# A two-layer decoder trunk on one core: output turns of the delta rule a step later, squares kept at norm boundaries, weight splits elsewhere

## What is computed

```python
def rms_norm(x, w):
    return x * lax.rsqrt(jnp.mean(x * x, axis=-1, keepdims=True) + NORM_EPS) * w

for layer in range(2):
    h = h + 0.5 * rms_norm(swiglu(rms_norm(h, nw[0]), gate0, up0, down0), nw[1])
    hn = rms_norm(h, nw[2])
    mix = even_mixer(hn, ...) if layer == 0 else odd_mixer(hn, ...)   # both end in "@ w_out"
    h = h + rms_norm(mix, nw[3])
    h = h + 0.5 * rms_norm(swiglu(rms_norm(h, nw[4]), gate1, up1, down1), nw[5])
return h[:, 16:]

# a part of even_mixer: the gated delta rule, four heads of 128, over a scan of chunks
def step(s, xs):
    attn_n, u_n, w_n, qd_n, kd_n, gl_n = xs
    v_new = u_n - w_n @ s
    o = qd_n @ s + attn_n @ v_new
    s = s * gl_n[..., None, None] + kd_n.T @ v_new
    return s, o                       # later: rms_norm(o, norm_w) * silu(z)
```

## Time and profile before

| | |
|---|---|
| median of 3 runs | 2191.31 us (2188.11 to 2193.72) |
| profiled execution, its own time | 2191.5 us |
| its span, first to last instruction | 2189.7 us |
| PE busy | 2145.0 us (98%), 16006 matmuls |
| DVE busy | 1010.7 us (46%) |
| ACT busy | 763.9 us (35%) |
| POOL busy | 100.1 us (5%) |
| mean granted clock of PE | 0.992 |

### The profile page before, as it was taken

The page is one execution under the profiler, slowest core; times in us unless marked ns, Lnnn a source line. Parts: engine busy times, 40 slices in busy tenths (PEclk is TensorE's granted clock), DMA queues, the critical chain, the costliest instruction groups (busy, mean ns, idle before and its releaser), DMA issues.

```text
span 2189.7 us, 38299 instructions
## 1 busy us (share of the span) xinstructions
PE 2145.0 (98%) x16006; PEld 2026.2 (93%) x16006; DVE 1010.7 (46%) x1390; ACT 763.9 (35%) x1259; POOL 100.1 (5%) x97
## 2 busy tenths in 40 slices
PE   8999999999999999999999999999999999999998
PEld 7999999998998999999999999999998788888887
DVE  6444422667485464444236444412663346444423
ACT  5222222346435542223234222322453454222322
POOL 0000000100050200000000000000000020000000
PEclk9999999999999999999999999999999999999999
DMA  4333333321110223334313332431322122333232
GB/s 128 95 90 94 98 107 85 77 74 49 49 30 1 76 79 88 94 89 119 93 56 87 88 94 87 118 93 51 94 78 59 40 70 85 95 96 96 96 106 77
DMA packets 328974, 179.69 MB, mean 82 GB/s; under 512 B 15849, under 2 KB 323344, under 8 KB 328878
## 3 DMA queue, kind: packets, MB, share of 16 engines
q1 hardware_dynamic: 327520, 175.30, 27.4%
q0 software_dynamic: 1024, 2.86, 0.5%
q10 hardware_dynamic: 334, 0.14, 0.0%
HBM read 176.16 MB, written 2.12 MB: 81 GB/s over the span
## 4 chain that ended last, share of the span: by engine, by line
PE 93%; DVE 4%; ACT 1%; issue 1%; DMA 0%; DVEq 0%; SPq 0%; ACTq 0%
PE psum L608 69%; PE psum L620 10%; PE psum L808 6%; DVE w_hl L523 1%; PE psum L2390 1%; PE psum L1858 1%; PE psum L2929 1%; PE psum L1870 0%; DMA stage<-ffn_w_gate 0%; PE psum L2945 0%; PE psum L2940 0%; DVE rinv L1374 0%; PE psum L674 0%; PE psum L698 0%; PE psum L2449 0%
## 5 line engine op out<-in xcount | busy, mean ns | idle before, releaser
L608 PE MATMUL psum<-x_hl,w_hl 128*128 128x264 f32 (+1 forms) x9120 | 1243.5, 298 | 7.2 <-DVE w_hl L523 6.0
L608 PEld LDWEIGHTS psum<-x_hl,w_hl 128*128 128x128 f32 x9120 | 1184.6, 189 | 59.1 <-issue 7.9
L523 DVE TENSOR_TENSOR w_hl<-stage,w_hl 128x1024 fp32r<-128x1024 f32 (+1 forms) x310 | 398.5, 1285 | 346.6 <-ACT w_hl L516 346.6
L516 ACT ACTIVATE w_hl<-stage 128x1024 fp32r<-128x1024 f32 (+1 forms) x310 | 339.5, 1096 | 217.4 <-PE psum L608 95.7
L608 PE MATMUL psum<-acts,w_hl 128*128 128x264 f32 x2376 | 288.9, 284 | 0.0
L608 PEld LDWEIGHTS psum<-acts,w_hl 128*128 128x128 f32 x2376 | 288.6, 188 | 0.0
L1416 DVE TENSOR_TENSOR t_both<-psum,rinv 128x528 f32<-128x528 f32 (+1 forms) x88 | 61.9, 703 | 304.4 <-PE psum L608 304.4
L1228 ACT ACTIVATE acts<-t_both 128x528 f32 (+3 forms) x88 | 56.7, 644 | 401.2 <-DVE t_both L1419 401.2
L620 PE MATMUL psum<-x_hl,w_hl 128*128 128x264 f32 (+1 forms) x1344 | 173.8, 289 | 6.9 <-DVE w_hl L523 4.6
L620 PEld LDWEIGHTS psum<-x_hl,w_hl 128*128 128x128 f32 x1344 | 168.0, 191 | 9.8 <-DVE w_hl L523 5.0
L1410 DVE TENSOR_TENSOR t_both<-psum,rinv 128x528 f32<-128x528 f32 (+1 forms) x88 | 61.9, 703 | 181.3 <-PE psum L608 181.1
(11 more groups left out here) (347 smaller groups left out, 1294.7 us busy)
## 6 DMA issues: line engine op xcount, KB each, us to landing
stage<-ffn_w_gate SPq DMA_DIRECT2D x88, 512.0 KB, 3.7
stage<-ffn_w_up SPq DMA_DIRECT2D x88, 512.0 KB, 3.7
stage<-ffn_w_down SPq DMA_DIRECT2D x48, 704.0 KB, 4.6
stage<-odd_w_in SPq DMA_DIRECT2D x24, 512.0 KB, 3.7
stage<-ffn_w_down SPq DMA_DIRECT2D x22, 512.0 KB, 3.4
stage<-even_w_in SPq DMA_DIRECT2D x18, 512.0 KB, 3.7
stage<-even_w_out SPq DMA_DIRECT2D x8, 512.0 KB, 3.5
stage<-odd_w_out SPq DMA_DIRECT2D x8, 512.0 KB, 3.5
```

Of the source, the lines that this page charges most:

```text
L516: act.activation(weights(core.w_hl[:, slot.ring, 0, :], *kind), weights(core.stage[:, slot.stage, :], *kind), ACT.Copy).then_inc(core.w_hi, 1)
L523: dve.tensor_tensor(weights(core.w_hl[:, slot.ring, 1, :], *kind), weights(core.stage[:, slot.stage, :], *kind), weights(core.w_hl[:, slot ...
L608: op = pe.matmul(out, lhs, moving[:, moved, kt, t0:t0 + n], start=first and part + moved == 0, stop=last and part == 1)
```

## The change

Four things, in the functions that the diff names.

1. At every boundary, `pre_sum` of part 1 is made after channel tile 6 of slots 0 to 2 (`PRE_SUM_KT`), before the last 9 matmuls of that loop, not after them.
2. At the two boundaries after "out": PE takes channel tiles 0 to 3 of slot 0, then 0 to 3 of slot 1, then 4 and 5 of each, then 6 and 7 (`first_order`); it waits for slot 1's weights only when it comes to slot 1; part 1's sums stand after unit 14 and its spread after unit 20; `pre_sum` of part 0 comes after slot 2. The squares of pairs 1 to 3 go into `in_squares`, where each keeps its place, and DVE adds all three after the last remainders. The third weight split of part 0 comes after pair 3; the fourth stands before the wait for part 1's spread.
3. Delta rule: the output turn of chunk c-1 stands after the inner product of chunk c on PE; ACT copies the new values before it scales the output of chunk c-1; DVE gates chunk c-2 where it gated c-1, and before the state's additions; the remainders of the attention's output are all made after the loop.
4. The decay of the last chunk's queries moves from `chunk_gates` to just before the last 128-token chunk's first inverse, and the weight split at item 4 moves to item 10.

```diff
 SUMS_UNIT, SPREAD_UNIT = 4, 9
+FIRST_UNITS = {"down": (4, 9), "out": (14, 20)}
+PRE_SUM_KT = 6
+
+def first_order(kind):
+    groups = [[0, 1, 2, 3], [4, 5], [6, 7]] if kind == "out" else [[kt] for kt in range(DT)]
+    return [(u, kt) for group in groups for u in range(2) for kt in group]
...
+def pair_squares(core, phase, pair):
+    return core.in_squares[:, 2 * pair:2 * pair + 2, :] if phase.kind == "out" else core.t_both
...
-    pe.wait_ge(k.w_lo, slots[1].count())
+    out = norm.phase.kind == "out"
+    sums_unit, spread_unit = FIRST_UNITS[norm.phase.kind]
...
+    pe.wait_ge(k.w_lo, slots[0].count())
     pe.wait_ge(k.part_out, norm.late0 + L)
...
-    for kt in range(DT):
+    for u, kt in first_order(norm.phase.kind):
+        if u == 1 and kt == 0:
+            pe.wait_ge(k.w_lo, slots[1].count())
         pe.wait_ge(k.x_lo, x0 + kt + 1)
-        for slot in slots[0:2]:
-            one(slot, kt, 0)
...
-    pre_sum(k, pe, norm, 0)
+        one(slots[u], kt, 0)
+        factors()
+    if not out:
+        pre_sum(k, pe, norm, 0)
     for slot in slots[2:]:
         pe.wait_ge(k.w_lo, slot.count())
         for kt in range(DT):
             one(slot, kt, 0)
+            factors()
+        if out and slot is slots[2]:
+            pre_sum(k, pe, norm, 0)
     pe.wait_ge(k.pre_root, norm.part0 + 1)
     for kt in range(DT):
         pe.wait_ge(k.x_lo, x0 + DT + kt + 1)
         for slot in slots[0:RING - 1]:
             one(slot, kt, 1)
-    pre_sum(k, pe, norm, 1)
+        if kt == PRE_SUM_KT:
+            pre_sum(k, pe, norm, 1)
...
-            if pair >= 2:
+            if pair >= 2 and phase.kind == "down":
                 act.wait_ge(k.part_h_added, q * (DT // 2 - 1) + pair - 1)
-            squares = square_sums(k, norm, part) if pair == 0 else k.t_both[:, :, t0:t0 + n]
+            squares = square_sums(k, norm, part) if pair == 0 else pair_squares(k, phase, pair)[:, :, t0:t0 + n]
...
+SPLITS_AFTER = {"down": {0: 1, 1: 2, 2: 3}, "out": {0: 1, 1: 2, 3: 3}}
...
+        if part and phase.kind == "out":
+            split_ahead(k, dve, split_lo, norm.next, 0, 0)
         dve.wait_ge(k.part_spread, q + 1)
...
-            if part == 0 and pair < RING - 1:
-                split_ahead(k, dve, split_lo, phase, last, pair + 1)
-            if part and pair == 0:
+            if pair and phase.kind == "down":
+                add_squares(pair)
+            if part == 0 and pair in SPLITS_AFTER[phase.kind]:
+                split_ahead(k, dve, split_lo, phase, last, SPLITS_AFTER[phase.kind][pair])
+            if part and pair == 0 and phase.kind == "down":
                 split_ahead(k, dve, split_lo, norm.next, 0, 0)
+        for pair in range(1, DT // 2 if phase.kind == "out" else 1):
+            add_squares(pair)
...
+    if c < NBLK:
+        queries_decayed(e, dve, c)
...
-LAST_TILE_AT = 4
+LAST_TILE_AT, LAST_SPLIT_AT = 4, 10
...
+        for half in range(2):
+            pe.wait_ge(e.v_new, 2 * c + half)
+            if c < NBLK:
+                state_part(c, half)
+        inner_part(c)
         if c == 1:
...
         output_turn(k, e, pe, c - 1)
-        for half in range(2):
-            pe.wait_ge(e.v_new, 2 * c + half)
-            if c < NBLK:
-                state_part(c, half)
-        inner_part(c)
...
     for c in CHUNK_ORDER:
+        if c == NBLK:
+            queries_decayed(e, dve, NBLK)
         if c != EARLY:
             first_inverse(k, e, dve, c)
...
+        if j == LAST_SPLIT_AT:
+            split_ahead(k, dve, split_lo, mix.phase, LAST_SLOT // RING, LAST_SLOT % RING)
...
-        if c == NBLK:
-            swa_lo(0)
-            swa_lo(1)
+        if c >= 2:
+            gated(c - 2)
...
-        if c:
-            gated(c - 1)
-    for kt in range(2, DT // 2):
+    for kt in range(DT // 2):
         swa_lo(kt)
+    gated(NBLK - 1)
     out_mean(NBLK)
```

More of the change, by code:

```diff
@@ L1348, in add, with add_squares @@
             dve.tensor_tensor(h, h, f[:, 2 * pair:2 * pair + 2, t0:t0 + n], ALU.add).then_inc(k.h_new, 2)
+        def add_squares(pair):
+            dve.wait_ge(k.part_h_sq, q * (DT // 2) + pair + 1)
+            if pair >= 2:
+                dve.wait_ge(k.part_h_added, q * (DT // 2 - 1) + pair - 1)
+            sums = square_sums(k, norm, part)
+            dve.tensor_tensor(sums, sums, pair_squares(k, phase, pair)[:, :, t0:t0 + n], ALU.add)\
+               .then_inc(k.part_h_added, 1)
         scale_f(0)
```

51 lines of the change are left out of this document (26 added, 25 removed).

## The result

The changed kernel takes 2170.83 us (median of 5 runs, 2166.49 to 2175.14); the kernel before took 2192.78 us beside it (5 runs). The ratio, which is taken over the single runs and not from the two medians, is 0.9907, 95% interval 0.9894 to 0.992: 20.4 us less, 17.5 to 23.2. The profiled execution took 2170.83 us, its span is 2169.1. Forecast was 2173.4, 18.1 less. Of the 31 runs of the kernel before in the third set of experiments one took 2725.46 us at a mean granted clock of 0.721, and the ratios leave it out.

The account below looks back on a forecast made before the run. PE was busy 98% of the span, so only its idle and slow-clock time could be won: 5.5 + 7.2 + 2.3 + 3.1 = 18.1 us off 2191.5 gave 2173.4 us, range 2167.5 to 2182.5.

Parts of the forecast that it names:

- B: At the two boundaries after "out", the reordered start cuts the split wait and slow clock: 3.6 us each, 7.2 us.
- D: In the inversion, moving the decay and the weight split removes waits and slow clock: 3.1 us, bounds 0 and 3.6.
- A: `pre_sum` of part 1 nine matmuls earlier at five boundaries, its chain starting 1.1 us sooner each: 5.5 us.
- So 4.5 us are lost, the wait and the slow clock together: Start after "out": 12.56 us against 8.04 after "down", the loss put on slot 1's split wait and the slow clock.
- C: In the delta rule, output turn a step later and new values copied first: 2.3 us, bounds 0 and 3.9.
- Net to there: -0.5 us: Moving the decay in the inversion: one PE wait shrinks 0.6 us, another of some 1.1 us comes before the fourth chunk's inverse.
- Rival 2: POOL holds DVE in the inversion, the split at item 10 costs 4.1 us, D gives 0: 2176.5 us, chance 0.10.
- 1: The slow clock goes elsewhere, three new half-clock stretches outside the touched places: 2178.5 us, chance 0.20.
- 3: After "out", PE waits for remainders of channel tiles 4 to 7 or in part 1: 2177.0 us, chance 0.10.
- 4: Only C fails, as PE reaches the output turn before its scaling is done: 2175.7 us, chance 0.04.
- 5: Fourth split's weights land late after "out", DVE stands, PE runs dry: 2200.8 us at 12 us late, chance 0.01.
- 6: The trace puts the waits down wrongly and only A works: 2186.0 us, chance 0.03.

Follow-up runs that it names:

- third set of experiments: Follow-up on what varies and what pays in C and D, four kernels run beside the kernel before, which took 2190.08 us (31 runs).
- after_again: The changed kernel once more, unaltered: 2170.66 us, ratio 0.9916 to the kernel before.
- decay_late: The changed kernel with the decay of the last chunk's queries at item 14 of the inversion: 2168.15 us, ratio 0.9905 to the kernel before.
- c_alone: The kernel before with only C (output turn a step later, new values copied first, gating a chunk later): 2189.55 us, ratio 0.9994.
- d_again: The kernel before with only D (decay and weight split moved), run a second time: 2188.99 us, ratio 1.0001.
- after: The changed kernel with all four parts, as first measured and profiled: 2170.83 us, ratio 0.9907 to the kernel before.
- before_again: The kernel before once more, unaltered: 2191.20 us, ratio 1.0011.
- turn_only: The kernel before with C's order on PE and DVE, but ACT still scaling the last chunk's output before copying new values: 2195.34 us, ratio 1.003.

## Why the prediction was right

**The sum.** 2173.4 was forecast from the profiled execution of before; 2170.83 came, the interval of the ratio holds 18.1. The touched pieces gave 17.9. That these two agree so well is in part luck: at the two boundaries after "out" the profile of before had as little harm from the slow clock as any of seven profiles. With B and D at their means the pieces give 5.5 + 11.1 + 2.7 + 2.0 = 21.3 us. Measured were 20.4 (17.5 to 23.2) and, with `after_again`, 18.4 (14.9 to 21.7); both intervals hold 18.1 as well as 21.3. One bound of the range is added up wrongly: one stretch more and 2 us less from B and D make 2177.1, not 2178.

**A** was exact: 1.1 us at each of the three boundaries after "down". The chain was the limit, and as long as before (774.01 - 768.46 = 5.55 us), and the wait for the root fell inside the nine matmuls. Before L608 0.5 to 0.7 us stayed by the weight loads, from which the forecast had its 0.7, and 0.3 to 0.5 by the matmuls. Alone it measured 4.4 us (2.2 to 6.4) for 5.5.

**B** was exact in size on this profile (3.7 and 3.6 us with A's 1.1 taken off, for 3.6 each), and the two small waits left (0.43 and 0.32 us for 0.4 and 0.3) were the ones named. The margin of DVE's additions was 0.9, for 0.6. What failed is the mechanism in the step "So 4.5 us are lost, the wait and the slow clock together", and in "I price it alike" for the other. The 4.5 us were lost on that profile, but to two waits: the slow clock there cost nothing, since PE next waited for ACT's copy of part 1 (0.63 us in the same timeline, 1.8 where the clock stayed high, and passed over in the forecast). The change removes that wait too, by setting part 1's sums later. The true loss has a fixed part, 41.3 - 37.6 = 3.7 and 40.3 - 36.7 = 3.6 us, and a part by the slow clock behind the second wait, 0 to 3.4, mean 1.4 and 2.4 at the two. So the term was mis-sized by the runs' mean: 11.1, not 7.2. The upper bound of 4.5 each was too low; it came from one execution. Which of the slow stretches a run gets was chance here, so that 7.2 came out on this pair of profiles is luck in that part.

**C**: 2.66 us in place of 2.3. The 0.3 us before each state's update were 0.26 in step 1 and below 0.1 in 2 and 3 (the step of 5.2 us was forecast), 0.56 before the last inner product. The wait of 0.4 us that the third slot of "out" should wait did not come: that piece is 40.14 for 40.10.

**D**: 2.5 us for 3.1, on this profile. The step "Net to there: -0.5 us" was 0.5 too kind: with the decay (1.25 us) ahead of it the fourth chunk's inverse took 1.77 us beside POOL's mask (1.25 in `decay_late`), and PE waited 1.59 us, not 1.1. The split's own gain, 1.9 us, was the 0.23 + 1.71 of the two waits, as the forecast had it before it took off the 0.5; net of the decay's 1.0 it is 0.9, for 1.45. The 1.7 us of slow clock were booked as sure, and come five times in seven. At item 10 the split took 1.94 us with no stall of PE, inside the 1.2 to 2.7 named; POOL was busy for 1.69 of the 2.20 us around it. At item 4 it took 4.10 with POOL busy all the time, and elsewhere 1.2. Rival 2 (4.1 us at item 10) was wrong for this. The Trainium skill, GPSIMD Engine Reference, section 8 (Key points), says that GpSimd contends with VectorE's instructions that have two SBUF inputs; the three times agree with it.

**The rivals.** 1 happened in part: stretches came and went in the untouched pieces, -1.0 us in layer 1, +4.8 before the inversion, the balance to the better side. The two profiles of before have the three stretches at 517, 551 and 585 us at the same microsecond, and `c_alone`, `d_again` and `after` have none of them with the same instructions there. The Trainium skill, TensorE: Matmul & The Clock Gate, Part 1, says that the monitor behind the clock runs free of the kernel and that the number of slow matmuls varies from run to run; that the stretches come and go agrees with it, while their three places stay the same here. "I am wrong if the half-clock stretches are as many as before": there are 2 besides the end in after, 8 in before, 2 to 4 in the other profiles with B, and 4 to 7 in the other ones without. 3 did not happen; 4 did not; 5 was far off, the weights being there 3.7 us before DVE wanted them; 6 falls with the single parts.

## What to carry to other kernels

Cut the timeline at the bounding engine's own instructions and compare pieces: they repeat to 0.1 us where medians of the same kernel differ by 1 or 2, and they tell what each edit did. They do not tell what the time will be where the clock varies: C's and D's pieces are shorter by 2.7 and 2.5 us, and neither alone gave a gain clear of the noise. Take a stall's price from several executions, and look at what the engine waits for next: time lost ahead of another wait is free, time lost behind it is not. When work is moved out of one engine's wait, move what ends that wait first (C's copy), or the work is only added; and don't put a short instruction ahead of the one that the bounding engine waits for, if it can go where the queue has room (the decay at item 14, 1.7 us).

## What the runs showed of the hardware that I had not expected

The clock drop behind a stall is not fixed. Behind the same 2.3 us wait at the start after "out" PE ran at 1.2 GHz for some 3.4 us at once (before), for about as long but only behind its next wait (`before_again`), or for some 10 us from the first wait on (`d_again`, `turn_only`). Behind the same 1.55 us wait of the inversion the clock dropped in five of seven profiles and stayed high in two. The removal of such a wait is then worth its idle time surely, and 0 to 3.4 us more by chance.

An instruction of DVE with two SBUF operands is slow beside POOL, but not in proportion to the time for which POOL runs beside it. The 128x1024 split took 1.2, 1.94 or 4.10 us, the 128x512 decay 1.40, 1.25 or 0.67, and the 0.67 of `decay_late` had POOL beside it for all but the first 0.05 us. What fits is when POOL's instructions begin and end. POOL's masks beside the decay in before, beside the split in before (two in one row), and beside the decay in `decay_late` (two in one row):

```profile
621.28 1.29 POOL L2357 TENSOR_TENSOR dn_v<-dn_a,dn_masks 128x512 f32<-128x512 f32 x1 [2.02 <-DVE dn_a L2211]
635.23 2.48 POOL L2357 TENSOR_TENSOR dn_v<-dn_a,dn_masks 128x512 f32<-128x512 f32 x2
```

```profile
642.53 3.08 POOL L2401 TENSOR_TENSOR dn_wide<-dn_a,dn_masks 128x512 f32<-128x512 f32 x2 [0.30 <-PE psum L2434]
```

In before the decay (621.72 + 1.40 = 623.12) ends 0.55 us after the mask that was running when it began (621.28 + 1.29 = 622.57), and the split (634.70 + 4.10 = 638.80) 1.09 us after the end of the masks beside it (635.23 + 2.48 = 637.71), both a little less than they take alone. In `decay_late` the decay began 0.05 us ahead of the mask and took its 0.67 us, and the two masks took 3.08 us, where two took 2.48 above. So it looks as if one of the two engines goes on and the other stands until that instruction has ended. This is read from these rows, and no run tested it. The subtraction of the inversion (L2650), which has one operand in PSUM, took 0.65 us at 630.15 in before with POOL busy throughout and 0.69 at 645.32 with POOL idle.
